# Weight sums of the block products: from VectorE to adding transfers, and the fourth output-matrix unit by block products in quarters two and three

## What is computed

```python
def sq_relu_mlp(xn, w_in, w_out):       # w_in 1024 x 4096, w_out 4096 x 1024
    h = jax.nn.relu(xn @ w_in)
    return (h * h) @ w_out

for i in range(DEPTH_2):                # 2 layers
    ...
    h = h + mix
    h = h + sq_relu_mlp(rms_norm(h, norm_mlp_g[i]), mlp_w_in[i], mlp_w_out[i])
```

## Time and profile before

| | |
|---|---|
| median of 3 runs | 1870.73 us (1869.96 to 1871.71) |
| the profiled execution | 1871.36 us |
| its span, first to last instruction | 1869.6 us |
| TensorE's granted clock, mean over the span | 0.998 |
| busy: PE, DVE, ACT, POOL | 1858.5, 1369.3, 944.1, 87.4 us |
| DMA | 179.34 MB, mean 96 GB/s |

### The profile page before, as it was taken

One profiled execution on the slowest core, in us unless ns is written; L12 is line 12 of the kernel. 1 busy time (PEld: TensorE's weight loads), 2 busy tenths in 40 slices (PEclk: granted clock), 3 DMA queues, 4 the chain that ended last, 5 costly groups with the idle time before them and its releaser, 6 DMA issues.

```text
span 1869.6 us, 28250 instructions
## 1 busy us (share of the span) xinstructions
PE 1858.5 (99%) x10603; PEld 1546.0 (83%) x10603; DVE 1369.3 (73%) x1870; ACT 944.1 (50%) x1206; POOL 87.4 (5%) x84
## 2 busy tenths in 40 slices
PE   9999999999999999999999999999999999999998
PEld 7788878888888887877888898988778788989897
DVE  7767775677357667556577898987788658789887
ACT  6392464555133344444543554555667744445464
POOL 0010021000000021000100000000110010000000
PEclk9999999999999999999999999999999999999999
DMA  6223122332322234222233223234232133233321
GB/s 242 90 85 125 44 68 68 104 98 68 112 90 91 74 105 134 68 82 68 90 99 98 96 92 113 92 112 149 88 104 71 59 101 102 82 107 99 105 91 68
DMA packets 146802, 179.34 MB, mean 96 GB/s; under 512 B 3581, under 2 KB 140669, under 8 KB 144256
## 3 DMA queue, kind: packets, MB, share of 16 engines
q1 hardware_dynamic: 143296, 160.44, 26.4%
q0 software_dynamic: 3104, 17.10, 2.9%
q10 hardware_dynamic: 288, 0.26, 0.0%
HBM read 173.48 MB, written 2.20 MB: 94 GB/s over the span
## 4 chain that ended last, share of the span: by engine, by line
PE 92%; DVE 5%; ACT 2%; DMA 1%; issue 0%; DVEq 0%; SPq 0%; ACTq 0%
PE bank L1059 22%; PE bank L1061 22%; PE bank L1060 22%; PE bank L1496 4%; PE bank L1498 4%; PE bank L1497 4%; PE bank L1187 2%; PE bank L1801 2%; PE bank L1783 1%; PE bank L1193 1%; DVE w_lo L2061 1%; DMA raw<-in_mlp_w_out 1%; PE bank L1672 1%; PE bank L1673 1%; PE bank L1674 1%; DVE w_lo L1897 1%
## 5 line engine op out<-in xcount | busy, mean ns | idle before, releaser
L1059 PE MATMUL bank<-n_hi,w_hi 128*128 128x512 f32 x1054 | 424.7, 403 | 1.3 <-DVE w_lo L1897 1.3
L1061 PE MATMUL bank<-n_hi,w_lo 128*128 128x512 f32 x1054 | 417.9, 396 | 0.0
L1060 PE MATMUL bank<-n_lo,w_hi 128*128 128x512 f32 x1054 | 416.7, 395 | 0.0
L1891 ACT ACTIVATE w_hi<-raw 128x2048 fp32r<-128x2048 f32 (+2 forms) x115 | 215.0, 1870 | 342.1 <-PE bank L1061 337.5
L1897 DVE TENSOR_TENSOR w_lo<-raw,w_hi 128x2048 fp32r<-128x2048 f32 (+2 forms) x121 | 271.2, 2241 | 105.5 <-ACT w_hi L1891 103.4
L1060 PE MATMUL bank<-ff_lo,w_hi 128*128 128x512 f32 x752 | 297.2, 395 | 0.0
L1061 PE MATMUL bank<-ff_hi,w_lo 128*128 128x512 f32 x688 | 273.0, 397 | 0.0
L1059 PE MATMUL bank<-ff_hi,w_hi 128*128 128x512 f32 x688 | 271.5, 395 | 1.0 <-DVE ff_lo L2199 0.8
L1059 PEld LDWEIGHTS bank<-n_hi,w_hi 128*128 128x128 f32 x1054 | 198.0, 188 | 54.2 <-issue 5.0
L1060 PEld LDWEIGHTS bank<-n_lo,w_hi 128*128 128x128 f32 x1054 | 198.1, 188 | 48.9 <-issue 2.9
L1061 PEld LDWEIGHTS bank<-n_hi,w_lo 128*128 128x128 f32 x1054 | 197.9, 188 | 46.6
(11 more groups left out here) (455 smaller groups left out, 3111.1 us busy)
## 6 DMA issues: line engine op xcount, KB each, us to landing
raw<-in_mlp_w_in SPq DMA_DIRECT2D x32, 1024.0 KB, 5.4
raw<-in_mlp_w_out SPq DMA_DIRECT2D x32, 1024.0 KB, 5.1
raw<-in_w_up SPq DMA_DIRECT2D x22, 1024.0 KB, 5.0
raw<-in_w_units SPq DMA_DIRECT2D x14, 1024.0 KB, 4.8
raw<-in_a_w_qkv SPq DMA_DIRECT2D x12, 1024.0 KB, 5.1
raw<-in_b_w_qkv SPq DMA_DIRECT2D x12, 1024.0 KB, 5.1
b_bias<-bias_table POOLq DMA_DIRECT2D x16, 448.0 KB, 4.5
raw<-in_w_down SPq DMA_DIRECT2D x8, 768.0 KB, 4.4
```

The costliest lines, as they stand in the source:

```text
L1059: nc.tensor.matmul(b[:, :], w_hi[:, j % 2, cols], hi, start=start, stop=False)
L1060: nc.tensor.matmul(b[:, :], w_hi[:, j % 2, cols], lo, start=False, stop=False)
L1061: return nc.tensor.matmul(b[:, :], w_lo[:, j % 2, cols], hi, start=False, stop=final)
L1891: act.activation(w_hi[:, s, cols], raw[:, s, cols], ACT.Copy).then_inc(hi_ready, 1)
```

## The change

1. The host lays the two MLP matrices of the second block out by units, and within a unit by the four 128-column, alternate-row blocks (`in_blocks`, `BLOCK_ORDER`), so that a block is 512 contiguous columns. The first of them is needed in the sums only, so a block unit's own load is now 768 KB instead of 1 MB.
2. POOL makes S1 to S4 of all block units with DMAs from DRAM to DRAM, two copies and three transfers that add to what is there, into a new DRAM tensor `weight_sums` (34 units of 1 MB, `SUM_UNITS`). Each step waits for the one before. The units are made in four stretches of POOL's queue: 12 after the norm before the first block's MLP, 4 after the first attention's part, 12 after the norm before layer 0's MLP, and 6 after the norm before layer 1's.
3. SP loads the sums: per block unit two more DMAs of 512 KB (`block_loads`), each after a wait until its place is free (`sums_home_free`) and, ahead of both, until the sums are made. DVE's three sum instructions go.
4. Unit 3 of the output matrix is by block products (LATE) in quarters two and three (m = 1, 2, 5, 6). T1's high part then lies in the free first blocks of the two `raw` buffers, since T4's place stays in use.
5. Signs in the T and operand sums are changed to suit sums made by adding only; the number of instructions stays. Banks are swapped in quarter three (`flipped`).

```diff
+BLOCK_ORDER = ((1, 0), (0, 0), (0, 1), (1, 1))
...
+        def has_late(m):
+            return m % 4 in (1, 2)
...
+        SUM_SETS = ((0, 12), (12, 16), (16, 28), (28, 34))
+        SUM_STEPS = (2, 1, 1, 1)
...
+        def block_loads(sp, ph):
+            m, is_out = block_phases[ph]
+            for j in range(4):
+                u = j + 2 * is_out
+                sp.wait_ge(lo_ready, ph.u0 + j - 1)
...
+                sp.dma_start(raw[:, j % 2, SEQ:4 * SEQ], t["mlp_out" if is_out else "mlp_in"][4 * m + j, :, SEQ:4 * SEQ]).then_inc(
+                    w_loaded[j % 2], 16)
+                sp.wait_ge(sums_made, 16 * sums_issued[SUM_ROW[m, u]])
+                for op in ("S23", "S14"):
+                    sums_home_free(sp, m, op, u)
+                    to, cols = sum_piece(op, u), slice(0, 2 * SEQ) if op == "S23" else slice(2 * SEQ, 4 * SEQ)
+                    sp.dma_start(to, t["weight_sums"][SUM_ROW[m, u], :, cols]).then_inc(sums_loaded[sums_place(u), op], 16)
...
+            def copied(row):
+                v, to = source(row), sums(row)
+                pool.dma_start(to[:, 0:2, :], v[:, 1:2, :].broadcast_to([P, 2, SEQ])).then_inc(sums_made, 16)
+                pool.dma_start(to[:, 2:4, :], v[:, 2:4, :]).then_inc(sums_made, 16)
+
+            def first_added(row):
+                pool.dma_start(sums(row)[:, 1::2, :], source(row)[:, 0:1, :].broadcast_to([P, 2, SEQ]), accum_op=ALU.add).then_inc(sums_made, 16)
+
+            def second_added(row):
+                pool.dma_start(sums(row)[:, 0:1, :], sums(row)[:, 3:4, :], accum_op=ALU.add).then_inc(sums_made, 16)
+
+            def third_added(row):
+                pool.dma_start(sums(row)[:, 2:3, :], sums(row)[:, 0:1, :], accum_op=ALU.add).then_inc(sums_made, 16)
...
             norm_pool(pool, 1)
+            weight_sums(pool, *SUM_SETS[0])
             pool.wait_ge(at("bias_stored"), 16)
             attention_a_pool(pool)
+            weight_sums(pool, *SUM_SETS[1])
             norm_pool(pool, 4)
+            weight_sums(pool, *SUM_SETS[2])
             attention_b_pool(pool)
             norm_pool(pool, 6)
+            weight_sums(pool, *SUM_SETS[3])
...
                     block_tensor(pe, m, DOWN)
-                    plain_down(pe, m, 3)
+                    if has_late(m):
+                        block_tensor(pe, m, LATE)
+                    else:
+                        plain_down(pe, m, 3)
...
         def burst_vector(dve, m):
             for u in range(UNITS):
                 more = u + 1 < UNITS
                 if more:
-                    if u:
-                        paired_sums(dve, m, u + 1)
-                    second_sum(dve, m, u + 1)
-                    fourth_sum(dve, m, u + 1)
                     piece_low(dve, m, "A1", u + 1)
...
-            if has_down(m):
-                paired_sums(dve, m, DOWN)
-                second_sum(dve, m, DOWN)
-                fourth_sum(dve, m, DOWN)
             unit_low(dve, m, UNITS - 1)
```

More of the change, by code:

```diff
@@ L42 @@
 UNIT = KD * GC
+SUM_UNITS = 34
 def t5_bucket(rel):
@@ L795, in build @@
             for m in range(4 * layer + 1, 4 * layer + 4):
-                for u in range(BLOCKS if has_down(m) else UNITS):
+                for u in blocks(m):
                     count(kept_count, m, u)
@@ L818, in piece_used, with sums_place, summed @@
             eng.wait_ge(at("piece_used"), piece_count[(m,) + piece])
-        def summed(eng, m, u, n):
-            eng.wait_ge(at("sums_ready"), sum_count[m, u, n])
+        SUM_ROW = {}
+        for m in range(8):
+            for u in blocks(m):
+                SUM_ROW[m, u] = len(SUM_ROW)
+        assert len(SUM_ROW) == SUM_UNITS
+        sums_loaded, sums_made = {(i, op): sem("%s_loaded%d" % (op, i)) for i in range(2) for op in ("S23", "S14")}, sem("sums_made")
+        SUM_SETS = ((0, 12), (12, 16), (16, 28), (28, 34))
+        SUM_STEPS = (2, 1, 1, 1)
+        sums_issued = [sum(SUM_STEPS) * (row + 1) for row in range(SUM_UNITS)]
+        def sums_place(u):
+            return u % 2 if u < UNITS else 0
+        def summed(eng, m, op, u):
+            i = sums_place(u)
+            eng.wait_ge(sums_loaded[i, op], 16 * sum(sums_place(v) == i and n <= SUM_ROW[m, u] for (_, v), n in SUM_ROW.items()))
         def places_free(eng, m, op, u):
             v = unit_index(m, u)
-            if u == 0:
+            if u == 0 and has_late(m - 1):
+                piece_used(eng, m - 1, {"A1": ("S4", DOWN), "A22": ("S3", LATE), "S23": ("A22", LATE), "S14": ("S4", LATE)}[op])
+            elif u == 0:
                 eng.wait_ge(w_used, v - (1 if op[0] == "A" else 0))
@@ L832, in places_free @@
                     eng.wait_ge(w_used, v - (0 if op == "A22" else 1))
+            elif u == LATE:
+                if op == "S23":
+                    piece_used(eng, m, ("S3", DOWN))
+                elif op == "S14":
+                    piece_used(eng, m, ("A11", LATE))
+                else:
+                    eng.wait_ge(w_used, p_dn[m].u0 + 2)
             elif op != "A22":
-                piece_used(eng, m, (PIECE_OF_OP[op][-1], u - 1))
+                piece_used(eng, m, (LAST_OF_OP[op], u - 1))
         def place(name, u):
-            return DOWN_PLACE[name] if u == DOWN else PLACE[name] + (u % 2 if name == "A22" else 0)
+            return DOWN_PLACE[name] if u == DOWN else LATE_PLACE[name] if u == LATE else PLACE[name] + (u % 2 if name == "A22" else 0)
         def places(v, op, u):
@@ L999, in shifts_of, with weight_sums, source, sums @@
             return bass.AP(tensor=table.tensor, offset=row * RB_COLS + at0, ap=[[1, P], [RB_COLS, rows], [1, n]])
+        def weight_sums(pool, first, last):
+            assert SUM_SETS[-1][1] == SUM_UNITS
+            def source(row):
+                m, u = list(SUM_ROW)[row]
+                v = t["mlp_in"][4 * m + u] if u < UNITS else t["mlp_out"][4 * m + u - 2]
+                return v.rearrange("p (b n) -> p b n", n=SEQ)
+            def sums(row):
+                return t["weight_sums"][row].rearrange("p (b n) -> p b n", n=SEQ)
+            def copied(row):
[8 more added lines that the diff above has]
+                pool.dma_start(sums(row)[:, 2:3, :], sums(row)[:, 0:1, :], accum_op=ALU.add).then_inc(sums_made, 16)
+            for row in range(first, last):
+                before = sums_issued[row] - sum(SUM_STEPS)
+                for n, part in zip(SUM_STEPS, (copied, first_added, second_added, third_added)):
+                    if before:
+                        pool.wait_ge(sums_made, 16 * before)
+                    part(row)
+                    before += n
+            pool.wait_ge(sums_made, 16 * before)
         def attention_a_pool(pool):
@@ L2050, in piece_high @@
             if op[0] == "S":
-                summed(act, m, u, {"S23": 2, "S14": 3}[op])
+                summed(act, m, op, u)
             else:
@@ L2374, in four_summed @@
             dve.wait_ge(norm_sq, 3 * NORM[n] + 1)
[L2375 removed]
+            done(dve, dve.tensor_tensor(two, two, scratch[:, 2:4, :], ALU.add), at("norm_pairs"), 2 * i + 1)
         def six_summed(dve, n):
@@ L2691, in down_scalar @@
             t_split_high(act, m, "T1")
-            split_hi(act, ph.u0 + 3, 1)
-            if m % 4 < 3:
-                for op in PIECE_OF_OP:
+            if has_late(m):
+                for op in ("A1", "A22", "S23"):
+                    piece_high(act, m, op, LATE)
+                first_kept(act, m, LATE)
+                piece_high(act, m, "S14", LATE)
+                for op in ("A1", "S23", "A22", "S14"):
                     piece_high(act, m + 1, op, 0)
+            else:
+                split_hi(act, ph.u0 + 3, 1)
         def burst_scalar(act, m):
```

237 lines of the change are left out of this document (135 added, 102 removed).

## The result

The changed kernel takes 1872.67 us, median of ten runs, where the kernel before took 1870.72 (ten runs beside it); the ratio is 1.0023, 95% interval 1.0013 to 1.0032. So it is the same to slightly slower, and I had forecast 1864.1. Its runs lie much further apart (1869.43 to 1880.64) than those of before (1869.71 to 1871.71), which suggests that something in it comes late by a different amount each time. The profiled execution took 1869.43 us, the shortest of the ten, so the trace shows the loss where it was smallest.

What follows compares the result with a forecast made beforehand. PE was taken to bound the kernel, busy 1858.5 of 1869.6 us, with DVE runner-up. Gains 4.6 + 2.0 + 0.3 - 0.3 = 6.6 us gave 1864.1 us from the 1870.7 median; 8-in-10 range 1862.6 to 1868.4.

Steps and rivals of the forecast that it cites:

- LATE at 1.15 us a unit, 4.6: Four plain output units become block units in m = 1, 2, 5, 6; each takes 1.15 us from PE, 4.6 us.
- The gaps of the six pairs, 2.0: Pairs of plain units behind the input units: removing DVE's sums lets ff_lo start sooner, gaining their 2.0 us excess over 22.40.
- what is late next: At the pairs of plain units, ACT's three steps become the latest work, but end before PE asks; no loss.
- its 0.3 us: In DOWN, PE waits for T1's low part from DVE; half of the 0.65 us excess counted as gained, 0.3 us.
- the 0.3 us taken off for LATE's deadlines: DVE's work before LATE's sixth piece fits with some 2 us to spare; 0.3 us in all deducted for possible delay.
- One of my signs of being wrong: In the block stages: the forecast is wrong if ACT waits for a transfer of sums.
- PE's idle time: Over the whole kernel, PE's total idle time would fall from 11.1 to about 9.5 us.
- POOL's stretches: POOL's four queue stretches: each unit of sums takes 21 us, so all four hide behind other work.
- bounds of 15.5 and 35.6: POOL's time for one unit of four chained steps: 15.5 us at least, 35.6 us at most.
- the room of the third stretch: From 345.78 us plus 25.7 to the bias tables' first reader, less 5.3 to land: 366 us, 30.5 a unit.
- POOL comes late: End of first or third stretch: above 30.5 us a unit PE stands still, 1924 us at 33, 1986 at 35.6; chance 0.08.
- Transfers crowd out the weights: Quarters two and three beside the third stretch: additions overload DMA engines, 9 us waiting at 5% over, 1873 us; chance 0.05.

Runs made afterwards that it cites:

- both loads moved: Changed kernel with its own stretches, but b_lam and the first two heads' b_bias loaded by ACT's queue, not POOL's: 1864.21 us, ratio 0.9965 to the kernel before.
- thirteen units: Changed kernel with thirteen units of sums in the third stretch and three in the second (12, 3, 13, 6): 1907.26 us, ratio 1.0183 to the kernel before.
- the second profile of the pairs: One more profiled run of the changed kernel with POOL issuing each step for two units of sums before the wait: 1870.17 us.
- the moved stretches: Changed kernel with two units of sums moved from third to second stretch (12, 6, 10, 6): 1863.79 us, ratio 0.9966 to the kernel before.
- the second profile: The changed kernel, unaltered, profiled once more: 1871.84 us.

## Why the prediction was wrong, point by point

**Right in the main: what TensorE would gain.** LATE at 1.15 us a unit, 4.6: DOWN and LATE together take 20.18 us where DOWN and a plain unit took 21.41, 1.23 a unit or 4.9, and the medians with and without LATE differ by 4.4. The gaps of the six pairs, 2.0: 2.2 without LATE, and all pairs at 22.40. In the timeline of DVE after the change the last `ff_lo` is released by ACT, as I had said of what is late next; it answers to the earlier trace rows.

```profile
1735.29 1.23 DVE L2312 TENSOR_TENSOR ff_lo<-scratch,ff_hi 128x1024 fp32r<-128x1024 f32 x1 [3.44 <-ACT ff_hi L2308]
```

Two small terms were wrong and cancelled. DOWN gave nothing of its 0.3 us: it takes 10.17 to 10.20 in all six quarters, as before. The loss stands at its sixth piece, the first two matmuls of which start 0.24 and 0.20 us behind the one ahead of each, where the pace is 0.12. The timeline of PE there, first before (quarter four of layer 1), then after (quarter two of layer 0):

```profile
1842.56 0.28 PE L1498 MATMUL bank<-t_mid,w_lo 128*128 128x256 f32 x1
1842.80 0.36 PE L1496 MATMUL bank<-t_far,w_hi 128*128 128x256 f32 x1
1843.00 0.28 PE L1497 MATMUL bank<-scratch_r,w_hi 128*128 128x256 f32 x1
```

```profile
1074.96 0.28 PE L1628 MATMUL bank<-t_mid,w_lo 128*128 128x256 f32 x1
1075.20 0.35 PE L1626 MATMUL bank<-raw_r,w_hi 128*128 128x256 f32 x1
1075.40 0.28 PE L1627 MATMUL bank<-scratch_r,w_hi 128*128 128x256 f32 x1
```

T1's low part on DVE ends 0.15 and 0.14 us ahead of that piece (1842.65, and 1075.06 after the change), and in LATE, where T1 has long been there, the gap is missing. So PE still waits for T1, as I had read it, but a lighter DVE did not bring it sooner: in quarter two of layer 0 it is ready 7.1 us into DOWN before and after. And the 0.3 us taken off for LATE's deadlines weren't needed: LATE takes 9.99, below the 10.08 that I had priced it at. Measured sum in the block stages 6.95, forecast 6.6. One of my signs of being wrong did come, without a cost: ACT waited nine times, 24.5 us in all, for a transfer of sums in the changed kernel, and PE did not. DVE ended 58.5 us lighter and not 53, since LATE costs it 5.1 us a unit (1310.8 less 1290.3 without LATE) and not 6.2. PE's idle time did not fall to 9.5 us, as I had put it: it is 10.9 without the lateness. Of the 2.0 us of gaps only 0.8 had stood in the profile before as idle time.

**Wrong, the step "POOL's stretches", first in its price.** I gave a unit 5.3 + 5.3 + 3.4 + 3.4 us and a fifth for the loads beside it, 21 us, inside bounds of 15.5 and 35.6. It is 26.5 in the first stretch and 29.9 to 31.0 in the third. The additions are 4 to 5 us of that; the rest is that copies between places in DRAM beside the weights took 22.1 and 24.9. All my rows were copies with a tile in SBUF at one end or both the earlier trace rows, and no run parts what the place in DRAM costs from what the load beside it costs. The estimate by the Trainium skill (DMA: Bandwidth & Descriptors, "Anatomy of one DMA"), 12.8 us, was further off. Its 3.2 us for 512 KB is near the 3.4 of POOL's four transfers of that size before the change, but the sums' transfers of 512 KB took 6.8 to 7.0, and 6.3 to 6.4 with plain copies.

**Wrong, the same step, in its slack.** I took the room of the third stretch up to the first reader of `b_bias` and reached 30.5 us a unit. But `b_lam` is issued first and read first: DVE was ready for it at 1271.44, it needs 3.42 us to land, and 1.6 us of DVE's wait of 4.74 cost PE nothing (PE waited 3.16). So the last issue without loss is at 1269.6, and the limit (1269.6 - 914.5) / 12 = 29.6 us a unit. Even the reader of `b_bias` had moved, since layer 0 ended 3.3 us earlier: with both loads moved it was released by PE at 1283.3, not 1286.3. Here the threshold of the queue is that of the first thing in it that anybody waits for, and the gain ahead of it brought it forward.

**The rival.** "POOL comes late" named the place, at 0.08, and a second place that was never late: the first stretch ended 31 us ahead of the norm. Its slope at one place, 12 us for each us of a unit, fits the 1 us of kernel per us of lateness that thirteen units showed; its threshold of 30.5 would have said no loss at 29.9. It lacked the slow clock, 3 us at the first lateness. With a price of 21 us I held a margin of 9.5 us a unit to be safe; the bounds themselves, 15.5 to 35.6, put the threshold well inside, and a chance of a third would have been nearer. "Transfers crowd out the weights" came about with two units side by side, and with one it made PE wait 1.4 us at most. The Trainium skill (the same page, "Issuing engines are not separate DMA queues") says that transfers issued from SP and POOL run on the same 16 engines and interleave, and the second profile of the pairs agrees: SP's load of 512 KB that took 6.0 us in the changed kernel took 10.5 beside two of POOL's units.

**The sum, rebuilt.** 1870.7 - 6.95 is 1863.8, which the moved stretches measured. The lateness adds 6.2 us in the profiled run and about 1 us for every us that POOL ends later (38.1 for 37.98 with thirteen units, 2.4 for 3.05 in the second profile), and the median of 1872.67 asks for 8.9, an issue of `b_lam` at 1272.76 + 2.7 = 1275.5; the second profile has it at 1275.81, in a run of 1871.84. No run of the group of 1878 to 1881 was profiled; that POOL ended near 1281 to 1284 in them is worked out from this line and not seen.

**Left open.** Why POOL's pace differs by 1 us a unit from run to run was not tried. The two groups of runs, in the changed kernel and with `b_lam` moved, look as if the pace took one of two values (29.9 to 30.3 us a unit in four profiles, 31.0 in the fifth), and five profiles can't show it. Nor is it known how much of a step is waiting for completion: pairs show only that two units cost 1.5 times one.

## What to carry to other kernels

When work is moved onto an idle queue, look up the first thing in that queue behind it that anybody waits for, and take the room from that reader, shortened by what the change gains ahead of it. Price a chain of transfers by rows of the same kind under the same load; if none exists, do not let the middle of wide bounds stand for the answer when the threshold lies within them. Where a kernel's runs suddenly scatter, look for such a threshold: one profile shows one draw, and moving a unit of work or the load behind it tells more than a second look.

## What the runs showed of the hardware

- An adding transfer from DRAM to DRAM costs more than a copy of the same size: 5.3 against 3.8 us for 256 KB, and the engines' share is higher by 0.11 in both stretches. Its issue on POOL also takes longer: 827 to 837 ns against 528 to 531.
- After 3.2 us in which PE stood still, the granted clock was 0.53 for 6.7 us and then 1.00 again; after 41.2 us it was 0.50 up to 1323 and back at 1.00 by 1330. Beside the waits of 3.2, 6.3 and 41.2 us the three runs lost 3.0, 1.7 and 3.1 us more, so the price does not grow with the wait, and it is less where PE stands still in part of the slow stretch.
- Waits of PE of 0.6, 1.2 and 1.4 us in a block stage had no slow clock behind them; one of 3.3 us had.
